# Two edits in a two-block transformer kernel: the order of ScalarE's copies in the within-chunk stage, and position scores of two heads on half the rows each

## The chip, the cores and the metric

The kernel runs on one core of a Trainium2 chip. The metric is the device time of one execution in microseconds (us), median of three runs. One further execution was profiled; all rows of the trace come from it.

## What is computed

The reference is a pair of transformer blocks on 256 tokens of width 2048, all in float32. The first block runs two layers of convolution and windowed attention. The second has a RWKV-7 mixer (16 heads of 64) beside a multi-head latent attention (8 heads), an output projection, and a gated feed-forward network. The two edited stages are the latent attention and a part of the RWKV mixer:

```python
# latent attention, 8 heads: 128 content dimensions and 64 position dimensions
sc = (einsum('bqhd,bkhd->bhqk', q_nope[:, q0:q1], k_nope[:, :q1])
      + einsum('bqhr,bkr->bhqk', q_pe[:, q0:q1], k_pe[:, :q1])) * scale
p = softmax(where(causal, sc, NEG_INF))
out = einsum('bhqk,bkhd->bqhd', p, v[:, :q1])
# RWKV-7: one step a token
sa = einsum('bhvk,bhk->bhv', state, a_t)
state = state * w_t + sa * b_t + v_t * k_t
out_t = einsum('bhvk,bhk->bhv', state, r_t)
```

The kernel computes the RWKV recurrence in chunks of 32 tokens: within a chunk the recurrence becomes a triangular system that is solved ahead, and a few small products; then a short chain over 8 chunks carries the state.

## The kernel before

The program is one long sequence of stages. Each stage gives every engine its own list of instructions, and an engine goes through its lists without stopping between stages; order across engines comes from semaphores alone, each counted upwards and written by hand (`wait_ge`, `then_inc`). Nothing plans the order but the code itself. Most stages stream weights in units of 128x2048 float32: SyncE loads a unit, ScalarE rounds it (line 229), VectorE or GpSimd forms the rest (lines 234, 241), and TensorE multiplies both parts.

**Latent attention** (`phase_mla`, lines 1722 to 1830). A head's scores lie in one PSUM bank, `1 + h % 3`, so three heads can be there at once: 128 columns for the first 128 queries, 256 for the second. TensorE's `scores(h)` (lines 1744 to 1752) makes for each query block one product of the content part (line 1750, 128 rows) and one of the position part (line 1751). The rotated position keys are 64 dimensions; the position queries of two heads share the 128 rows of one tile (`qT[:, 8 + h // 2]`), so the keys stand in `k_pad` twice, for even heads on rows 0 to 63 and for odd heads on rows 64 to 127, and the other half is zero. Then:

- VectorE, `biased(h)`: waits for head h's scores and for the transposes of head h-2 (its buffer `smm` is used by turns), scales and masks (line 1804), takes maxima (lines 1806, 1807) and negates them (line 1808);
- ScalarE: exponentials and their sums (lines 1783, 1784);
- VectorE, `finished(h)`: reciprocals and normalisation (lines 1813 to 1815);
- TensorE: three transposes (line 1765), which ScalarE copies (line 1793), and the output product (line 1775), which VectorE stores (line 1819).

TensorE's list is: scores of heads 0 and 1, and then for n from 0: scores of head n+2, transposes of head n, output of head n-1. VectorE's list is `biased(n + 1)`, `finished(n)`, `store(n - 2)`. `scores(h)` waits from head 3 on until `biased(h - 3)` has read the bank.

**Within-chunk stage** (`phase_within`, lines 1838 to 2001). There are 16 items: 8 pairs of heads by 2 halves of the sequence. For item n TensorE does, in this order: the products `G` (line 1915), the four transposes of the tokens of item n+1 into bank 2 (line 1860), the solved products `aq` (line 1923, into bank 5), the scores of item n+1 (line 1871: three products for each of two heads, on 64 rows each), the outputs that use `aq` (lines 1932, 1934, 1936), and the small products of the four chunks (lines 1945, 1947, 1949). ScalarE copies `G` (line 1974), moves `held` to `step_n` for item n-1 (`step_out`, line 1968, which waits for VectorE), copies the tokens of item n+1 out of bank 2 (`tokens_read`, lines 1961 to 1963), and copies `aq` (line 1980). VectorE masks the scores (line 1878), reads bank 5 (lines 1990, 1991), and reads the small products (lines 1997, 1999).

Of the kernel before, what the change touches and what calls it, by code (L numbers as in the profile page):

```python
# [10 lines left out]
ACT = mybir.ActivationFunctionType  # L11
AX = mybir.AxisListType

P = 128
# [14 lines left out]
MLA_H, NOPE, ROPE, VH = 8, 128, 64, 128  # L29
# [116 lines left out]
def program(nc, xT, pT, weights, params, sinks, rel_bias, lora, positions, consts, onehot, band_mask, masks, inv_freq, table, chunk_mats, out):  # L146
    ctx = ExitStack()
    with ctx:
# [1577 lines left out]
        def phase_mla(u_next, following):  # L1726
            scale = (NOPE + ROPE) ** -0.5
            stage = Stage()

            @stage.gpsimd  # L1730
            def _(pool):
                pool.wait_ge(mm_done.sem, u_next)
                pool.memset(lower[:, 16:32, :], 0.0).then_inc(mx["cleared"].sem, 1)

            @stage.sync
            def _(sp):
                sp.wait_ge(*mx["cleared"](1))
                for c in range(4):
                    sp.dma_start(lower[32 * c:32 * c + 32, :, 32 * c:32 * c + 32],
                                 chunk_mats[32 * c:32 * c + 32, :, :].rearrange("i s t -> s i t")).then_inc(mx["sol_in"].sem, 16)  # L1740

            @stage.tensor
            def _(pe):
                def scores(h):
                    if h >= 3:
                        pe.wait_ge(*ml["biased"](h - 2))
                    for qb in range(2):
                        n = P + P * qb
                        dst = ps[:, 1 + h % 3, P * qb:P * qb + n]
                        pe.matmul(dst, qT[:, h, P * qb:P * qb + P], kT[:, h, 0:n], start=True, stop=False)  # L1750
                        mm = pe.matmul(dst, qT[:, 8 + h // 2, P * qb:P * qb + P], k_pad[:, h % 2, 0:n], start=False, stop=True)
                    mm.then_inc(ml["scores"].sem, 1)

                pe.wait_ge(ev_done.sem, u_next + 2)
                scores(0)
                scores(1)
                for n in range(MLA_H + 1):
                    if n + 2 < MLA_H:
                        scores(n + 2)
                    if n < MLA_H:  # L1760
                        pe.wait_ge(*ml["normed"](n + 1))
                        if n >= 2:
                            pe.wait_ge(*ml["probsT_read"](n - 1))
                        for x in range(3):
                            mm = pe.transpose(ps[:, 4 + n % 2, x * P:x * P + P], smm[:, n % 2, x, :], ident[:, :])
                        mm.then_inc(ml["probsT"].sem, 1)
                    if n == MLA_H:
                        following.first_products(pe)
                    if n >= 1:
                        h = n - 1  # L1770
                        pe.wait_ge(*ml["probsT_read"](h + 1))
                        if h >= 2:
                            pe.wait_ge(*ml["stored"](h - 1))
                        for x, (q, k) in enumerate(((0, 0), (1, 0), (1, 1))):
                            mm = pe.matmul(ps[:, 6 + h % 2, q * P:q * P + P], vM[:, k, h * P:h * P + P], pTm[:, h % 2, x, :], start=k == 0, stop=k == q)
                        mm.then_inc(ml["outT"].sem, 1)

            @stage.scalar
            def _(act):
                def exps(h):  # L1780
                    s = st[:, h % 3, :]
                    act.wait_ge(*ml["biased"](h + 1))
                    act.activation(smm[:, h % 2, 0, :], smm[:, h % 2, 0, :], ACT.Exp, bias=s[:, 4:5], accum_out=s[:, 8:9])
                    act.activation(smm[:, h % 2, 1:3, :], smm[:, h % 2, 1:3, :], ACT.Exp, bias=s[:, 5:6], accum_out=s[:, 9:10]).then_inc(ml["exps"].sem, 1)

                exps(0)
                for h in range(MLA_H):
                    if h + 1 < MLA_H:
                        exps(h + 1)
                    act.wait_ge(*ml["probsT"](h + 1))  # L1790
                    if h >= 2:
                        act.wait_ge(*ml["outT"](h - 1))
                    act.activation(pTm[:, h % 2, :, :], ps[:, 4 + h % 2, 0:3 * P].rearrange("p (x k) -> p x k", x=3), ACT.Copy).then_inc(ml["probsT_read"].sem, 1)

            @stage.vector
            def _(v):
                link = dve_chain.start(v)

                def biased(h):
                    s = st[:, h % 3, :]  # L1800
                    v.wait_ge(*ml["scores"](h + 1))
                    if h >= 2:
                        v.wait_ge(*ml["probsT"](h - 1))
                    link(v.scalar_tensor_tensor(smm[:, h % 2, :, :], ps[:, 1 + h % 3, 0:3 * P].rearrange("p (x k) -> p x k", x=3), scale,
                                                causal[:, :, :], ALU.mult, ALU.add))
                    v.tensor_reduce(s[:, 0:1], smm[:, h % 2, 0, :], axis=AX.X, op=ALU.max)
                    link(v.tensor_reduce(s[:, 1:2], smm[:, h % 2, 1:3, :].rearrange("p x k -> p (x k)"), axis=AX.X, op=ALU.max))
                    v.tensor_scalar(s[:, 4:6], s[:, 0:2], -1.0, None, ALU.mult).then_inc(ml["biased"].sem, 1)

                def finished(h):  # L1810
                    s = st[:, h % 3, :]
                    v.wait_ge(*ml["exps"](h + 1))
                    link(v.reciprocal(s[:, 10:12], s[:, 8:10]))
                    v.tensor_scalar(smm[:, h % 2, 0, :], smm[:, h % 2, 0, :], s[:, 10:11], None, ALU.mult)
                    v.tensor_scalar(smm[:, h % 2, 1:3, :], smm[:, h % 2, 1:3, :], s[:, 11:12], None, ALU.mult).then_inc(ml["normed"].sem, 1)

                def store(h):
                    v.wait_ge(*ml["outT"](h + 1))
                    v.tensor_copy(y_mla[:, h, :], ps[:, 6 + h % 2, 0:T]).then_inc(ml["stored"].sem, 1)

                v.wait_ge(*mx["causal_in"](32))
                biased(0)
                for n in range(MLA_H + 2):
                    if n + 1 < MLA_H:
                        biased(n + 1)
                    if n < MLA_H:
                        finished(n)
                    if n == MLA_H:
                        following.first_mask(v)
                    if n >= 2:  # L1830
                        store(n - 2)
                link.end()
            return stage
# [8 lines left out]
        def phase_within(u_next):  # L1842
# [110 lines left out]
            @stage.scalar  # L1953
            def _(act):
                def tokens_read(n):
                    pair, sc = items[n]
                    y = n % 2
                    act.wait_ge(*wi["tok"](n + 1))
                    if n >= 2:
                        act.wait_ge(*wi["mn"](2 * (n - 1)))  # L1960
                    act.activation(tokA[:, y, :, 0:DH], ps[:, 2, 0:P].rearrange("p (h d) -> p h d", h=2), ACT.Copy)
                    act.activation(tokV[:, y, :], ps[:, 2, P:2 * P], ACT.Copy)
                    act.activation(chunk_ends[:, pair, sc, :, :], ps[:, 2, 2 * P:4 * P].rearrange("p (x d) -> p x d", x=2), ACT.Copy).then_inc(wi["tok_read"].sem, 1)

                def step_out(n):
                    pair, sc = items[n]
                    act.wait_ge(*wi["mn_read"](2 * n + 2))
                    act.activation(step_n[:, pair, sc, :, :], held[:, :, :], ACT.Copy).then_inc(wi["held"].sem, 1)

                tokens_read(0)  # L1970
                for n, (pair, sc) in enumerate(items):
                    y = n % 2
                    act.wait_ge(*wi["G"](n + 1))
                    act.activation(tokA[:, y, :, DH:P], ps[:, 5, 0:P].rearrange("p (h d) -> p h d", h=2), ACT.Copy).then_inc(wi["G_read"].sem, 1)
                    if n:
                        step_out(n - 1)
                    if n + 1 < len(items):
                        tokens_read(n + 1)
                    act.wait_ge(*wi["aq"](n + 1))
                    act.activation(aq[:, y, :, :], ps[:, 5, P:3 * P].rearrange("p (h d) -> p h d", h=2), ACT.Copy).then_inc(wi["aq_read"].sem, 1)  # L1980
                step_out(len(items) - 1)

            @stage.vector
# [487 lines left out]
```

## Time and profile before

| what | value |
|---|---|
| median of three runs | 2248.16 us (2246.68 to 2249.49) |
| the profiled execution | 2245.08 us, of which 2243.3 us are the span of the profile |
| TensorE products, busy | 2197.8 us (98%), 14609 instructions |
| TensorE weight loads, busy | 1930.5 us (86%) |
| VectorE, busy | 1698.2 us (76%) |
| ScalarE, busy | 1068.6 us (48%) |
| GpSimd, busy | 550.0 us (25%) |
| latent attention | from 1260 to 1288 us of the span |
| within-chunk stage | from 1288 to 1357 us |

Two thirds of the span are the large products of the two blocks; the chain that ended last runs through TensorE for 86% of it. The two edited stages are 4% of the span. In rows of the timeline the first number is the start in us from the span's start, the second the duration in us; PE is TensorE's products, PEld its weight loads, DVE is VectorE, ACT is ScalarE. A float32 product appears as two records. A bracket gives the idle time of that engine just ahead and what ended it.

### The profile page before, as it was taken

Reading aid. Unit: us, or ns where it says so; the run is one execution under the profiler, and the core shown is the slowest. Engines: PE = TensorE matmul, PEld = TensorE weight load, DVE = VectorE, ACT = ScalarE, POOL = GpSimd, SP = SyncE. Lnnn points to the kernel's source line nnn. Section 1 sums busy time; section 2 is a strip of 40 time slices with the busy share of each in tenths; the row PEclk is TensorE's granted clock in tenths of the full one; section 3 lists DMA queues with packets and bytes.
Section 4 is the critical chain, followed back from the end, with each engine's and each line's share of the span. In section 5 each row is a group of like instructions: output and inputs, shape, how many; then the busy total and the mean of one; then the engine's idle time right before and its main releaser. Section 6 shows DMA issues by size and latency. Waiting matters only on the chain.

```text
span 2243.3 us, 38851 instructions
## 1 busy us (share of the span) xinstructions
PE 2197.8 (98%) x14609; PEld 1930.5 (86%) x14609; DVE 1698.2 (76%) x2879; ACT 1068.6 (48%) x1427; POOL 550.0 (25%) x226
## 2 busy tenths in 40 slices
PE   7999999999999999999999899999999999999997
PEld 6888888888888888899999887888888888888886
DVE  7688678885888588788878766788888885447886
ACT  5444464444545564556644633444444443334444
POOL 4676631018676530210001322100000000000011
PEclk9999999999999999999999999999999999999998
DMA  7445445555545355554445300555555555555554
GB/s 253 172 175 176 146 170 188 188 187 189 183 165 173 142 186 182 187 193 170 159 150 186 113 3 21 188 185 187 186 188 187 187 186 189 188 186 189 187 207 167
DMA packets 69032, 384.89 MB, mean 172 GB/s; under 512 B 15088, under 2 KB 22768, under 8 KB 23984
## 3 DMA queue, kind: packets, MB, share of 16 engines
q1 hardware_dynamic: 68912, 383.22, 48.3%
q8 instruction: 84, 1.38, 0.2%
q14 instruction: 36, 0.29, 0.0%
HBM read 380.02 MB, written 3.18 MB: 171 GB/s over the span
## 4 chain that ended last, share of the span: by engine, by line
PE 86%; DVE 5%; issue 3%; ACT 2%; POOL 1%; DMA 1%; SPq 0%; DVEq 0%; POOLq 0%; ACTq 0%
PE ps L259 44%; PE ps L260 24%; PE ps L262 3%; PE ps L247 3%; PE ps L248 2%; PE ps L249 2%; PE ps L878 1%; DVE low L234 1%; PE ps L859 1%; POOL ssq L1139 1%; DMA raw<-weights_dram 1%; PE ps L867 1%; DVE step_m L1997 1%; ACT whi L229 0%; PE ps L913 0%
## 5 line engine op out<-in xcount | busy, mean ns | idle before, releaser
L259 PE MATMUL ps<-opA,whi 128*128 128x512 f32 x2460 | 871.9, 395 | 0.3 <-DVE low L234 0.3
L260 PE MATMUL ps<-opA,low 128*128 128x256 f32 x2624 | 706.7, 279 | 0.2 <-DVE opA L996 0.2
L229 ACT ACTIVATE whi<-raw 128x2048 fp32r<-128x2048 f32 x346 | 660.2, 1909 | 76.3 <-DMA raw<-weights_dram 74.7
L234 DVE TENSOR_TENSOR low<-raw,whi 128x2048 fp32r<-128x2048 f32 x252 | 577.1, 2291 | 66.7 <-ACT whi L229 50.6
L259 PEld LDWEIGHTS ps<-opA,whi 128*128 128x128 f32 x2460 | 461.0, 187 | 106.2 <-issue 2.8
L241 POOL TENSOR_TENSOR low<-raw,whi 128x2048 fp32r<-128x2048 f32 x95 | 436.7, 4606 | 440.5 <-ACT whi L229 414.1
L259 PE MATMUL ps<-opB,whi 128*128 128x512 f32 x1380 | 497.1, 400 | 16.2 <-DVE opB L408 11.7
L260 PEld LDWEIGHTS ps<-opA,low 128*128 128x128 f32 x2624 | 492.0, 188 | 14.3 <-DVE opA L996 0.5
L260 PE MATMUL ps<-opB,low 128*128 128x256 f32 x1472 | 398.5, 281 | 0.0
L259 PEld LDWEIGHTS ps<-opB,whi 128*128 128x128 f32 x1380 | 260.9, 189 | 80.5 <-DVE low L402 10.4
L268 ACT ACTIVATE crossed<-ps 128x256 f32<-128x256 f32 x168 | 64.6, 384 | 513.7 <-PE ps L262 513.5
L260 PEld LDWEIGHTS ps<-opB,low 128*128 128x128 f32 x1472 | 278.7, 189 | 7.3
L717 DVE SCALAR_TENSOR_TENSOR ps<-a_in,par,ps 128x256 f32<-128x256 f32 x464 | 226.8, 489 | 14.6
L259 PE MATMUL ps<-act_hl,whi 128*128 128x512 f32 x672 | 236.5, 393 | 0.0
L1135 POOL MEMSET ssq<- 128x256 f32 (+1 forms) x4 | 1.5, 366 | 807.2 <-DVE t L988 677.1
L260 PE MATMUL ps<-act_hl,low 128*128 128x256 f32 x704 | 191.4, 279 | 0.0
L247 PE MATMUL ps<-opB,whi 128*128 128x256 f32 x560 | 161.8, 289 | 0.2 <-DVE ps L1442 0.2
L249 PE MATMUL ps<-opB,low 128*128 128x256 f32 x560 | 158.8, 284 | 0.0
L248 PE MATMUL ps<-opB,whi 128*128 128x256 f32 x560 | 158.5, 283 | 0.0
L259 PEld LDWEIGHTS ps<-act_hl,whi 128*128 128x128 f32 x672 | 125.9, 187 | 28.6
L260 PEld LDWEIGHTS ps<-act_hl,low 128*128 128x128 f32 x704 | 131.9, 187 | 2.9
L1139 POOL TENSOR_TENSOR ssq<-ssq,sq 128x256 f32<-128x256 f32 (+1 forms) x64 | 65.4, 1021 | 247.5 <-ACT sq L1052 182.6
(390 smaller groups left out, 2661.8 us busy)
## 6 DMA issues: line engine op xcount, KB each, us to landing
raw<-weights_dram SPq DMA_DIRECT2D x350, 1024.0 KB, 4.8
bias_t<-table_dram SPq DMA_DIRECT2D x16, 384.0 KB, 5.8
hT<-xT_dram SPq DMA_DIRECT2D x4, 512.0 KB, 9.0
out_dram<-hT SPq DMA_DIRECT2D x4, 512.0 KB, 2.9
lora_g<-lora_dram SPq DMA_DIRECT2D x1, 1024.0 KB, 4.9
p_in<-pT_dram SPq DMA_DIRECT2D x2, 256.0 KB, 5.1
lora_wa<-lora_dram SPq DMA_DIRECT2D x1, 512.0 KB, 5.6
chunk_mats_dram<-compact SPq DMA_DIRECT2D x4, 128.0 KB, 3.1
```

Source lines behind the costliest of these rows:

```text
L229: act.activation(whi[:, v % RING, :], raw[:, v % RING, :], ACT.Copy).then_inc(hi_done.sem, 1)
L234: v_.tensor_tensor(wlo(v % RING, 0, width), raw[:, v % RING, 0:width], whi[:, v % RING, 0:width].bitcast(F32), ALU.subtract).then_inc(lo_d ...
L241: pool.tensor_tensor(wlo(v % RING), raw[:, v % RING, :], whi[:, v % RING, :].bitcast(F32), ALU.subtract).then_inc(lo_done.sem, 1)
L247: pe.matmul(dst, whi[:, s, w0:w0 + P], op[:, k, 0:T], start=start, stop=False)
L248: pe.matmul(dst, whi[:, s, w0:w0 + P], op[:, k, T:2 * T], start=False, stop=False)
L249: return pe.matmul(dst, wlo(s, w0, w0 + P), op[:, k, 0:T], start=False, stop=stop)
L259: pe.matmul(*cross, start=start, stop=False)
L260: mm = pe.matmul(ps[:, b, 0:T], wlo(s, w0, w0 + P), op[:, k, 0:T], start=False, stop=False)
L262: mm = pe.matmul(*cross, start=False, stop=True)
L268: act.activation(crossed[:, b, :], ps[:, b if bank is None else bank, T:2 * T], ACT.Copy).then_inc(read.sem, 1)
L717: link(v.scalar_tensor_tensor(y, taps, w, y, ALU.mult, ALU.add))
L1139: pool.tensor_tensor(total, total, part, ALU.add).then_inc(summed.sem, 1)
```

## The change

In latent attention TensorE's `scores` now makes two heads in one piece: the content products of both, then the position products of both, each of these on the 64 rows that hold the head's queries and keys, and one signal for the pair. A pair is issued at even steps only. VectorE's wait counts pairs. In the within-chunk stage ScalarE's copy of `aq` stands ahead of the token copies of the next item.

```diff
             def _(pe):
-                def scores(h):
-                    if h >= 3:
-                        pe.wait_ge(*ml["biased"](h - 2))
+                def scores(pair):
+                    for h in (2 * pair, 2 * pair + 1):
+                        if h >= 3:
+                            pe.wait_ge(*ml["biased"](h - 2))
                     for qb in range(2):
                         n = P + P * qb
-                        dst = ps[:, 1 + h % 3, P * qb:P * qb + n]
-                        pe.matmul(dst, qT[:, h, P * qb:P * qb + P], kT[:, h, 0:n], start=True, stop=False)
-                        mm = pe.matmul(dst, qT[:, 8 + h // 2, P * qb:P * qb + P], k_pad[:, h % 2, 0:n], start=False, stop=True)
+                        dst = [ps[:, 1 + (2 * pair + x) % 3, P * qb:P * qb + n] for x in range(2)]
+                        for x in range(2):
+                            pe.matmul(dst[x], qT[:, 2 * pair + x, P * qb:P * qb + P], kT[:, 2 * pair + x, 0:n], start=True, stop=False)
+                        for x in range(2):
+                            r = slice(64 * x, 64 * x + 64)
+                            mm = pe.matmul(dst[x], qT[r, 8 + pair, P * qb:P * qb + P], k_pad[r, x, 0:n], start=False, stop=True)
                     mm.then_inc(ml["scores"].sem, 1)
 
                 pe.wait_ge(ev_done.sem, u_next + 2)
                 scores(0)
-                scores(1)
                 for n in range(MLA_H + 1):
-                    if n + 2 < MLA_H:
-                        scores(n + 2)
+                    if n % 2 == 0 and n + 2 < MLA_H:
+                        scores(n // 2 + 1)
...
                 def biased(h):
                     s = st[:, h % 3, :]
-                    v.wait_ge(*ml["scores"](h + 1))
+                    v.wait_ge(*ml["scores"](h // 2 + 1))
...
                     if n:
                         step_out(n - 1)
+                    act.wait_ge(*wi["aq"](n + 1))
+                    act.activation(aq[:, y, :, :], ps[:, 5, P:3 * P].rearrange("p (h d) -> p h d", h=2), ACT.Copy).then_inc(wi["aq_read"].sem, 1)
                     if n + 1 < len(items):
                         tokens_read(n + 1)
-                    act.wait_ge(*wi["aq"](n + 1))
-                    act.activation(aq[:, y, :, :], ps[:, 5, P:3 * P].rearrange("p (h d) -> p h d", h=2), ACT.Copy).then_inc(wi["aq_read"].sem, 1)
                 step_out(len(items) - 1)
```

## Rows read from the trace of the kernel before

**Rows 1.** Waits, both stages: engine and line, releaser: us in total, times, longest

```profile
PEld ps L1932 <- ACT aq L1980: 4.6, 15, 0.4
```

**Rows 2.** Timeline of a steady item of the within-chunk stage

```profile
1320.32 0.96 DVE L1878 TENSOR_TENSOR scm<-ps,msk 128x768 f32<-128x768 f32 x1 [1.32 <-PE ps L1871]
1320.38 0.20 PEld L1932 LDWEIGHTS ps<-scm,aq 128*64 128x64 f32 x4 [0.30 <-ACT aq L1980]
...
1321.51 0.28 DVE L1991 COPY kk<-ps 128x128 f32<-128x128 f32 x1
...
1321.95 0.52 PEld L1915 LDWEIGHTS ps<-tokV,scm 128*128 128x128 f32 x4
...
1322.97 0.71 PE L1923 MATMUL ps<-tokA,lower 128*128 128x128 f32 x4
...
1323.32 0.42 ACT L1968 ACTIVATE step_n<-held 128x256 f32<-128x256 f32 x1 [0.40 <-DVE held L1999]
1323.61 0.30 PEld L1871 LDWEIGHTS ps<-uS,a_gate 64*128 64x128 f32 x4
...
1324.16 0.39 PE L1871 MATMUL ps<-uS 64*128 64x128 f32 x4
1324.22 0.40 ACT L1980 ACTIVATE aq<-ps 128x256 f32<-128x256 f32 x1
...
1324.66 0.20 PEld L1932 LDWEIGHTS ps<-scm,aq 128*64 128x64 f32 x4 [0.30 <-ACT aq L1980]
```

**Rows 3.** Timeline of the first item and the start of the second

```profile
1288.97 0.71 PE L1923 MATMUL ps<-tokA,lower 128*128 128x128 f32 x4
...
1290.16 0.39 PE L1871 MATMUL ps<-uS 64*128 64x128 f32 x4
1290.48 0.20 PEld L1932 LDWEIGHTS ps<-scm,aq 128*64 128x64 f32 x4
...
1291.67 0.28 DVE L1991 COPY kk<-ps 128x128 f32<-128x128 f32 x1
...
1292.06 0.52 PEld L1915 LDWEIGHTS ps<-tokV,scm 128*128 128x128 f32 x4
...
1293.09 0.71 PE L1923 MATMUL ps<-tokA,lower 128*128 128x128 f32 x4
```

**Rows 4.** Timeline of the start of latent attention, heads 0 and 1

```profile
1260.35 0.49 PE L1750 MATMUL ps<-kT,qT 128*128 128x128 f32 x2 [0.65 <-DVE small L1619]
...
1260.67 0.39 PE L1751 MATMUL ps<-k_pad,qT 128*128 128x128 f32 x2
...
1260.89 0.60 PE L1750 MATMUL ps<-kT,qT 128*128 128x256 f32 x2
...
1261.33 0.59 PE L1751 MATMUL ps<-k_pad,qT 128*128 128x256 f32 x2
...
1262.04 0.56 DVE L1804 SCALAR_TENSOR_TENSOR smm<-ps,causal 128x384 f32<-128x384 f32 x1 [1.75 <-PE ps L1751]
...
1263.28 0.17 DVE L1808 TENSOR_SCALAR st<-st 128x2 f32<-128x2 f32 x1
...
1265.46 0.31 PEld L1765 LDWEIGHTS ps<-ident,smm 128*128 128x128 f32 x3 [1.32 <-DVE smm L1815]
```

**Rows 5.** Timeline of two later heads

```profile
1268.23 0.31 PEld L1765 LDWEIGHTS ps<-ident,smm 128*128 128x128 f32 x3 [1.31 <-DVE smm L1815]
...
1269.29 0.39 PE L1750 MATMUL ps<-kT,qT 128*128 128x128 f32 x2
...
1271.00 0.31 PEld L1765 LDWEIGHTS ps<-ident,smm 128*128 128x128 f32 x3 [0.64 <-DVE smm L1815]
```

**Rows 6.** Busy by stretch: PE, PEld, DVE, ACT, POOL busy (instructions), PEclk granted clock, DMA share, GB/s

```profile
1401.00:1405.00 4.00, 1.79 (x10) 1.09 (x8) 3.93 (x8) 1.87 (x3) 0.00 (x0) 0.97 0.02 4
1405.00:1411.00 6.00, 5.70 (x17) 4.53 (x18) 3.18 (x7) 1.04 (x3) 0.00 (x0) 0.50 0.00 0
1278.00:1282.00 4.00, 2.28 (x15) 1.63 (x14) 3.45 (x13) 1.63 (x6) 1.02 (x2) 1.00 0.00 0
```

## The prediction

> **What bounds the kernel now.** I began with the page: TensorE is busy nearly everywhere, so outside the two edited stages the change can only move things in time. The stages are short: latent attention runs from about 1260 to 1288 us of the span, the within-chunk stage from there to 1357. I then asked who waits for whom in them, and read the timeline of one steady item, of the first item, and of the first heads.
>
> The waits name the target of the first edit: TensorE's weight loads of line 1932 wait for ScalarE's copy of `aq` 15 times, 4.6 us in all [rows 1]. The steady item shows why. The item repeats every 4.28 us (line 1932 at 1320.38 and at 1324.66). The solved products of line 1923 end at 1322.97 + 0.71 = 1323.68, but their copy (line 1980) starts only at 1324.22, because ScalarE first does `step_out` (line 1968, from 1323.32, held back by VectorE's `held`) and then three token copies. TensorE has meanwhile finished the next scores (1324.16 + 0.39 = 1324.55) and stands until 1324.66 [rows 2].
>
> In latent attention the chain is another one. One head follows another every 2.77 us (line 1765 at 1268.23 and 1271.00), and each time the transposes wait for VectorE's normalised probabilities; the bracket of the second row still has 0.64 us of idle load time [rows 5]. VectorE's next head waits for the transposes in turn, so VectorE, ScalarE's exponentials and three transposes make the cycle and the score products hide inside it. At the very start they don't: VectorE's line 1804 begins at 1262.04, when the scores of head 0, begun at 1260.35, are done [rows 4].
>
> **Edit 1, the order of ScalarE's copies.** Nothing is added or removed; three token copies move behind the `aq` copy. In the new order the `aq` copy can start once `step_out` is over (1323.32 + 0.42 = 1323.74) and the products have ended (1323.68), so it ends near 1324.13, 0.4 us before the scores do. ScalarE's wait for `aq` now stands ahead of the token copies. Who needs those: line 1915 of the next item, 1.57 us after line 1932 (1320.38, 1321.95) [rows 2]. The three copies take at most 0.9 us (1323.32 to 1324.22 holds them and line 1968), so they end by 1325.0; line 1915 then comes at 1324.48 + 1.57 = 1326.05, a microsecond later. Nothing new stalls there.
>
> What TensorE gets is not the whole idle time. After the last score product (64 rows of the array) comes line 1932 (128 rows, 64 columns), and the first item shows this step without a wait, since there `step_out` does not exist yet: last score group at 1290.16, line 1932 at 1290.48, 0.32 apart; in the steady item 1324.16 and 1324.66, 0.50 apart [rows 2, 3]. So 0.18 us an item is to be had and the rest belongs to the switch. The first item's own period agrees: line 1923 at 1288.97 and 1293.09, 4.12 against 4.28 [rows 2, 3].
>
> Would VectorE then take over? Line 1915 waits for its line 1991, which in the steady item ends at 1321.79, 1.47 after the mask of line 1878 began at 1320.32; line 1915 follows at 1321.95 [rows 2]. If that stayed, only 0.10 of the 0.18 would come. But in the first item, with line 1932 early, line 1991 runs from 1291.67 to 1291.95 and line 1915 starts at 1292.06, 1.58 after line 1932 as in the steady item (1.57), so VectorE isn't in the way [rows 3]. I take 0.18. It counts for items 2 to 14; item 1 has about half (its old period was shorter), item 0 had no wait, item 15 has no next tokens and no change. 13 x 0.18 + 0.09 = **2.4 us gained**. Bounds: 0 if something else takes the place, 4.6 if the whole wait goes.
>
> **Edit 2, scores two heads at a time.** Counts first. The 32 products stay 32; 16 of them (the position part) now use 64 rows each, two side by side. A 128-column product takes 0.22 us of the array (1260.67 to 1260.89), a 256-column one 0.44 (1260.89 to 1261.33) [rows 4]. A pair of heads is now 2 x 2 x (0.22 + 0.44) = 2.64 us. In the within-chunk scores, the same form (two heads on 64 rows each, two banks), a pair of 128-column products fits in one slot: three pairs start at 1323.61 and the last group starts at 1324.16, 0.11 + 2 x 0.22 later [rows 2]. So the new pair needs 1.32 for the 128-row products and 0.66 for the position products: 1.98.
>
> Against that stand changes of the array's form: 128 to 64 rows and back, twice a pair. Their price is in the steady item: line 1923's last product ends at 1323.68, lasting 0.28, so it began at 1323.40 and the next could have begun at 1323.51; line 1871's load begins at 1323.61 and is not hidden, which costs another 0.11 [rows 2]. That is 0.21, I take 0.20; four of them are 0.80. The pair costs **2.78 us against 2.64**: the side by side gains nothing on TensorE. The Trainium skill (TensorEngine Tiling, Theoretical Speedup) gives up to 2x for dimensions of at most 64, by which the pair would be 1.98 us; the same page says under Key Properties that a change of tiling mode drains the array. The rows above decide for the drain here.
>
> The larger cost is one of order: a pair's scores are signalled together, and TensorE does a pair in one piece at even steps.
> - Start: head 0's scores are ready after the whole pair. 0.11 for the first load, 1.98, three inner switches and the last record's tail: about 2.85 after 1260.35, at 1263.20 in place of 1261.92. Line 1804 moves from 1262.04 to 1263.32: **+1.28**.
> - Pair 1 must wait until head 0's biased scores have been read out of its bank (line 1808, 1263.28 + 0.17 + 1.28 = 1264.73) and then stands ahead of the first transposes. It starts at 1264.79 and lets the transposes go at 1264.79 + 2.78 = 1267.57. Before, they went at 1265.46 [rows 4]: 2.11 late, **0.83** beyond the start's share. What is queued behind TensorE's wait is just this: head 0's transposes, for which VectorE waits.
> - Pairs 2 and 3: the score products start 1.06 after a head's transposes (1268.23, 1269.29) [rows 5]. With 2.67 behind them (2.78 less the hidden first load) the next transposes go at 3.73 in place of 2.77: **0.96 each, 1.92**. At odd steps nothing is inserted and the 2.77 holds; that time doesn't give it back, as the chain runs through the transposes.
>
> Sum: 1.28 + 0.83 + 1.92 = **4.0 us lost**. Bounds: were the switches free, the start would cost 0.66, pair 1 another 0.14 and pairs 2 and 3 0.16 each, 1.1 together; were the 64-row pairs not side by side, each of the four pairs adds 0.66, 6.7 together. One signal a pair instead of two is nothing beside that. The zeroed half of `k_pad` is still written; its fill is unchanged. No queue but TensorE's and VectorE's waits is touched by this edit, and no DMA is moved.
>
> **Sum against the profile.** +4.0 - 2.4 = +1.6 us. The profiled execution took 2245.08 us (span 2243.3), 3.1 under the median of 2248.16; it would become 2246.7, and the median **2249.8**. A measurement of this kernel can tell about 0.2%, 4.5 us, from no change.
>
> **Rivals.**
> - *The clock falls* (chance 0.20). Between head 0's transposes and head 1's TensorE will now stand idle for about 2.2 us (2.77 less 0.55 of work), soon after 1.6 us of idling for pair 1. Of 4 us with 1.79 busy at 1401 the trace shows the end at a granted clock falling to 0.50, 1.2 GHz, and six busy microseconds stay there; 4 us with 2.28 busy at 1278 kept 1.00 [rows 6]. The new stretch from 1267 to 1271 has some 1.8 busy. At half clock, the transposes, the output products and pair 2 (0.33 + 0.66 + 1.98) take 3.0 longer on the path: +4.6, **2252.8**, slower than before. It decides only if the fall comes before pair 2. The Trainium skill (TensorE: Matmul & The Clock Gate, Part 1) has it that idling throttles and activity releases; that agrees with these rows.
> - *The 64-row pairs do not overlap* (0.08): +6.7 - 2.4 = +4.3, **2252.5**. Against: the score groups of line 1871.
> - *Edit 1 gives nothing* (0.10), VectorE's reads or the later token copies setting the same 4.28: +4.0, **2252.2**. Against: the first item.
> - *Switches cheap* (0.12): 1.1 - 2.4 = -1.3, **2246.9**. For it: a load of another row group might start early; against: the load of line 1871 begins only 0.07 before the recorded end of line 1923 [rows 2].
> - The case of the sum keeps 0.50.
>
> A gain over 0.2% would need 4.5 us, practically all of the wait and no loss in attention: 0.03. A loss over 0.2% is the clock case's upper part and pieces of the two before it: 0.17. The range takes in the rivals' times and the spread of the median: 2245.5 to 2254.0.
>
> **What would show it.** Right: in attention line 1804 first starts 1.2 to 1.4 us after its old place, and head-to-head distances alternate between about 2.8 and 3.7; line 1751 appears as 64-row groups; attention ends some 4 us later. In the within-chunk stage line 1932's wait for `aq` is gone but for item 15, the period is 4.10, and 16 items end 2.4 us nearer to their start. Wrong: a new wait before line 1915 or 1974, a period still at 4.28, distances in attention of 2.77 throughout, or a granted clock under 1.00 between 1260 and 1360.

## The result, and the profile after

The kernel after takes 2251.46 us, median of 20 runs (2248.67 to 2254.66). In the same series of runs the kernel before took 2246.49 us. The ratio is 1.0021, with a 95% interval of 1.0015 to 1.0028: 4.7 us slower, just over what the prediction called tellable. The profiled execution took 2250.74 us, its span 2248.9 us. The prediction started from 2248.16 us for the kernel before, the median of three runs; the 2246.49 is that of 20.

The page shows the same busy time on every engine as before within 4 us, so the loss is time in which TensorE waits or runs slowly:

```profile
span 2248.9 us, 38853 instructions
...
PE 2198.7 (98%) x14609; PEld 1930.6 (86%) x14609; DVE 1698.0 (76%) x2879; ACT 1072.2 (48%) x1427; POOL 548.5 (24%) x226
```

The waits of both stages (line numbers are three higher in the kernel after: 1926 was 1923, 1935 was 1932, 1768 was 1765). The first row is of the kernel before, the others are of the kernel after:

```profile
DVE smm L1804 <- PE ps L1765: 2.9, 6, 0.7
DVE smm L1807 <- PE ps L1768: 8.8, 6, 3.1
...
PEld ps L1752 <- DVE st L1811: 2.0, 1, 2.0
PEld ps L1755 <- issue: 1.9, 5, 0.7
...
PEld ps L1935 <- ACT aq L1981: 0.4, 1, 0.4
```

The last row answers to [rows 1]: 4.6 us in 15 waits became 0.4 in one, that of the last item. The others are new or larger: VectorE waits 8.8 us for transposes where it waited 2.9, and TensorE's loads wait once 2 us for bank 1. Ahead of five position products the loads stand idle for a time that the profile puts down to nothing; there the array changes its form, from products on 128 rows to products on 64.

A steady item of the within-chunk stage, to be held against [rows 2]:

```profile
1322.09 0.52 PEld L1918 LDWEIGHTS ps<-tokV,scm 128*128 128x128 f32 x4
...
1323.12 0.71 PE L1926 MATMUL ps<-tokA,lower 128*128 128x128 f32 x4
1323.44 0.42 ACT L1971 ACTIVATE step_n<-held 128x256 f32<-128x256 f32 x1 [0.38 <-DVE held L2002]
...
1323.87 0.39 ACT L1981 ACTIVATE aq<-ps 128x256 f32<-128x256 f32 x1
...
1324.31 0.39 PE L1874 MATMUL ps<-uS 64*128 64x128 f32 x4
...
1324.62 0.20 PEld L1935 LDWEIGHTS ps<-scm,aq 128*64 128x64 f32 x4
...
1325.82 0.28 DVE L1994 COPY kk<-ps 128x128 f32<-128x128 f32 x1
1326.21 0.52 PEld L1918 LDWEIGHTS ps<-tokV,scm 128*128 128x128 f32 x4
```

ScalarE's copy of the solved products ends at 1324.26, and line 1935 follows the scores by 0.31 us (1324.31, 1324.62) instead of 0.50. The item repeats after 4.12 us (1322.09, 1326.21). VectorE's line 1994 ends at 1326.10, 0.11 us ahead of the next line 1918, and no wait for it is on the list.

Latent attention's start and first transposes, to be held against [rows 4]:

```profile
1261.24 0.71 PE L1752 MATMUL ps<-kT,qT 128*128 128x128 f32 x4 [0.67 <-DVE small L1619]
1261.88 0.30 PEld L1755 LDWEIGHTS ps<-k_pad,qT 64*128 64x128 f32 x4
...
1262.30 1.13 PE L1752 MATMUL ps<-kT,qT 128*128 128x256 f32 x4
...
1263.36 0.30 PEld L1755 LDWEIGHTS ps<-k_pad,qT 64*128 64x128 f32 x4 [0.33 <-issue]
...
1264.19 0.56 DVE L1807 SCALAR_TENSOR_TENSOR smm<-ps,causal 128x384 f32<-128x384 f32 x1 [3.01 <-PE ps L1755]
...
1265.65 0.52 PEld L1752 LDWEIGHTS ps<-kT,qT 128*128 128x128 f32 x4 [1.99 <-DVE st L1811]
...
1266.88 2.07 PE L1752 MATMUL ps<-kT,qT 128*128 128x256 f32 x4
...
1268.89 1.18 PE L1755 MATMUL ps<-k_pad,qT 64*128 64x256 f32 x4
...
1270.00 0.31 PEld L1768 LDWEIGHTS ps<-ident,smm 128*128 128x128 f32 x3 [0.61 <-issue]
...
1272.77 0.31 PEld L1768 LDWEIGHTS ps<-ident,smm 128*128 128x128 f32 x3 [2.46 <-DVE smm L1818]
```

The first mask now comes 2.95 us after the first score (before: 1.69). Pair 0 takes what was reckoned, but pair 1 does not: its 256-column content products last 2.07 us where pair 0's lasted 1.13, and its position products 1.18. The busy time by stretch says why. Its columns are those of [rows 6]; the granted clock is the number ahead of the last two:

```profile
1261.00:1265.00 4.00, 2.83 (x16) 1.80 (x16) 0.84 (x5) 1.18 (x1) 1.44 (x1) 1.00 0.78 268
1265.00:1270.00 5.00, 4.34 (x16) 2.56 (x17) 2.42 (x10) 1.98 (x8) 0.00 (x0) 0.66 1.00 104
1270.00:1273.00 3.00, 0.78 (x7) 0.54 (x6) 1.95 (x7) 1.39 (x5) 0.00 (x0) 1.00 0.00 0
1273.00:1277.00 4.00, 4.00 (x20) 3.44 (x19) 2.28 (x8) 1.57 (x6) 0.00 (x0) 0.57 0.01 2
...
1290.00:1294.00 4.00, 3.50 (x17) 3.50 (x18) 1.92 (x7) 1.81 (x6) 0.00 (x0) 0.57 0.02 4
```

TensorE fell to half its clock, 1.2 GHz, three times between 1266 and 1294 us: in pair 1, in pair 2, and in the last output products. In the execution profiled before, the whole of both stages ran at 1.00:

```profile
1260.00:1360.00 100.00, 93.23 (x1561) 77.17 (x1561) 65.34 (x245) 41.12 (x139) 21.24 (x20) 1.00 0.11 29
```

### The profile page after: what moved, and what is told of

Same layout as the page of the kernel before. It is cut to its first block, busy times and chain, and to the rows that moved or that the text cites. A ratio compares the mean times of both kernels' runs of the same rounds, so it can differ in the third digit from the quotient of the medians.

```text
span 2248.9 us, 38853 instructions
## 1 busy us (share of the span) xinstructions
PE 2198.7 (98%) x14609; PEld 1930.6 (86%) x14609; DVE 1698.0 (76%) x2879; ACT 1072.2 (48%) x1427; POOL 548.5 (24%) x226
## 4 chain that ended last, share of the span: by engine, by line
PE 88%; DVE 4%; issue 3%; ACT 2%; POOL 1%; DMA 1%; SPq 0%; POOLq 0%; DVEq 0%; ACTq 0%
PE ps L259 44%; PE ps L260 24%; PE ps L262 3%; PE ps L247 3%; PE ps L248 2%; PE ps L249 2%; PE ps L878 1%; DVE low L234 1%; PE ps L859 1%; POOL ssq L1139 1%; DMA raw<-weights_dram 1%; PE ps L867 1%; PE ps L1874 1%; PE ps L1926 0%; PE ps L1918 0%
```

## Where the time went, by milestones

Each row is read from the timeline of one profiled execution; times are in us from the first score of attention. "Distances" are those of the loads of the transposes, head 0 to head 7. "Attention" is the time to item 0's solved products (line 1923 before), and "items" the time from there to the last `step_out`. "Kept busy" means that TensorE is given products that nobody needs in its idle stretches of attention (see e4).

| kernel | first mask | head 0's transposes | distances | attention | items |
|---|---|---|---|---|---|
| before | 1.69 | 5.11 | 2.77 2.77 2.76 2.77 3.22 2.77 1.15 | 28.62 | 68.09 |
| after | 2.95 | 8.76 | 2.77 5.27 2.77 3.71 3.21 2.77 1.77 | 37.13 | 66.00 |
| e1, copy order alone | 1.69 | 5.11 | 2.77 2.77 2.77 2.76 3.23 2.76 1.77 | 29.99 | 65.97 |
| e2, pairs alone | 2.95 | 7.17 | 2.76 5.29 2.77 3.71 3.22 3.12 1.76 | 36.02 | 68.19 |
| e3, pairs, full rows | 3.00 | 6.98 | 2.92 3.46 2.93 3.46 3.37 2.77 1.77 | 35.03 | 65.99 |
| e4, pairs, kept busy | 2.95 | 7.17 | 2.77 3.71 2.76 3.71 3.22 2.77 1.16 | 32.57 | 65.99 |
| e5, copy order, kept busy | 1.69 | 5.12 | 2.77 2.76 2.77 2.77 3.22 2.78 1.15 | 28.65 | 65.98 |
| e6, first heads single, kept busy | 1.69 | 5.91 | 2.77 3.71 2.76 3.71 3.22 2.77 1.16 | 31.31 | 65.96 |
| e7, 64 rows, one head | 2.28 | 6.40 | 2.76 3.04 3.04 3.04 3.22 2.77 1.15 | 30.72 | 65.97 |
| e8, full rows, kept busy | 3.00 | 6.97 | 2.93 3.46 2.92 3.47 3.38 2.77 1.16 | 32.36 | 65.97 |
| e9, as e5 in these stages | 1.69 | 5.11 | 2.77 2.77 2.77 2.77 3.22 2.77 1.16 | 28.63 | 65.97 |
| e10, e1 again | 1.69 | 5.11 | 2.76 2.77 2.76 2.77 3.22 2.77 1.15 | 28.63 | 65.97 |
| e11, pairs, busy at the start only | 2.95 | 7.17 | 2.76 3.71 2.76 3.71 3.22 2.77 1.77 | 33.89 | 65.97 |

So attention lost 8.5 us in the profiled execution (37.13 against 28.62), and the items gave 2.1 back (68.09, 66.00). That is 6.4 us more, while the two spans differ by 5.6 (2248.9 and 2243.3). The normalisation stage behind them gave about 1.2 back, since the clock fell there in the execution before ([rows 6]) and not in the one after; the account of e9 has the numbers. The experiments had to tell how the 8.5 divides into the order in pairs, the array's changes of form, and the clock.

Each ratio below is to runs of the kernel before in the same series, whose medians were 2246.49 us for the kernel after, 2246.75 for e1 to e4, 2247.28 for e5 to e8 and 2247.23 for e9 to e11. Ratios of different series can be compared, the medians only roughly. Most experiments have 10 or 11 runs, e2 has 5.

| kernel | ratio to before, 95% interval | median us |
|---|---|---|
| after | 1.0021 (1.0015 to 1.0028) | 2251.46 |
| e1, copy order alone | 0.9994 (0.9985 to 1.0003) | 2245.35 |
| e10, the same again | 0.9996 (0.9986 to 1.0005) | 2245.09 |
| e2, pairs alone | 1.0038 (1.0024 to 1.0051) | 2254.05 |
| e3, pairs, full rows | 1.0022 (1.0012 to 1.0031) | 2251.05 |
| e4, pairs, kept busy | 1.0008 (0.9999 to 1.0017) | 2248.56 |
| e11, pairs, busy at the start only | 1.0018 (1.0009 to 1.0027) | 2250.99 |
| e6, first heads single, kept busy | 0.9998 (0.9989 to 1.0007) | 2246.71 |
| e8, full rows, kept busy | 1.0008 (0.9999 to 1.0017) | 2248.89 |
| e7, 64 rows, one head at a time | 0.9999 (0.9990 to 1.0008) | 2246.53 |
| e5, copy order, kept busy | 0.9988 (0.9978 to 0.9997) | 2243.89 |
| e9, e5 and the norm stage kept busy | 0.9984 (0.9975 to 0.9993) | 2242.99 |

## The experiments

### e1 and e10: the copy order alone

The kernel before with only this edit:

```diff
+                    act.wait_ge(*wi["aq"](n + 1))
+                    act.activation(aq[:, y, :, :], ...)
                     if n + 1 < len(items):
                         tokens_read(n + 1)
-                    act.wait_ge(*wi["aq"](n + 1))
-                    act.activation(aq[:, y, :, :], ...)
```

> Edit 1 alone (ScalarE copies the solved products ahead of the next tokens; attention as before). Theory: the within-chunk items go from 4.28 to 4.12 us apart as in the kernel after, the stage is 2.1 us shorter and the whole kernel 2 us faster than before (ratio 0.9991). Rival: the shorter items only came with what the attention edit shifted, and the items stay at 4.28: no change. In attention the distance of the transposes stays 2.77 us and the granted clock 1.00.

> Edit 1 alone once more, for its interval beside e5 and e9 on the same chip. Theory: 2.1 us from the within-chunk stage, ratio 0.9991; the granted clock may fall at the end of attention, as it did in e1's trace. If e5 is really faster than this, the unneeded products in attention are worth about 1 us in the median.

The items are 4.12 us apart in both traces and the items' time is 65.97 us, 2.1 less than before. The rival, that the edit needs what attention shifted, is out. The ratios of 0.9994 and 0.9996 have the forecast 0.9991 in their intervals, and 1.0 too: the whole kernel's time alone would not have settled this; the items do. In e1's execution the clock fell at the end of attention, in the old order of heads:

```profile
1263.00:1285.00 22.00, 17.39 (x112) 14.28 (x112) 16.41 (x58) 11.29 (x36) 2.73 (x3) 1.00 0.30 73
1285.00:1289.00 4.00, 3.50 (x18) 3.50 (x19) 1.92 (x7) 1.80 (x6) 0.00 (x0) 0.57 0.02 4
```

It cost 1.4 us of attention (29.99 against 28.62). The same kernel as e10 had no fall there, nor had the execution of before:

```profile
1258.00:1300.00 42.00, 36.69 (x421) 30.80 (x421) 28.41 (x100) 19.09 (x64) 16.91 (x19) 1.00 0.18 39
```

The fall is a matter of the execution, not only of the kernel.

### e2: the pairs alone

The kernel after with ScalarE's two lines back in the old order.

> Edit 2 alone (pairs of heads, position products on 64 rows; ScalarE's order as before). If the two edits simply add: before plus 5.0 plus 2.1, so about 7 us slower (ratio 1.0031), with the first output products of the within-chunk stage 8 to 9 us later after the first score than before. Rival, the edits interact (edit 1 gave more because of what edit 2 left late): the loss is only about 5 us.

The ratio is 1.0038, the loss 8.5 us; 7 lies in the interval, 5 (ratio 1.0022) does not. So the edits add, as far as five runs can tell. The wait of edit 1 is back at its old size, and attention was hit by the clock twice:

```profile
PEld ps L1935 <- ACT aq L1983: 4.7, 15, 0.4
```

```profile
1271.00:1274.40 3.40, 3.40 (x13) 2.17 (x11) 1.74 (x8) 0.99 (x4) 0.00 (x0) 0.50 0.01 2
...
1284.60:1291.40 6.80, 5.68 (x26) 5.39 (x27) 3.88 (x14) 2.95 (x10) 0.00 (x0) 0.50 0.01 2
```

The first low stretch lies in pair 2 and makes the distance from head 1's to head 2's transposes 5.29; the same distance from head 3 to head 4, with pair 3 at full clock, is 3.71.

### e4: the pairs, with TensorE kept busy

```diff
                 scores(0)
+                pe.wait_ge(hi_done.sem, u_next + 1)
+                gaps = (0, 8, 0, 6, 0, 6, 6, 0)
+                following.keep_running(pe, 6, 0)
...
                     if n < MLA_H:
+                        following.keep_running(pe, gaps[n], 0)
                         pe.wait_ge(*ml["normed"](n + 1))
```

`keep_running` is the kernel's own: it multiplies weights that are there into a bank that nobody reads.

> The kernel after, with TensorE fed unneeded 512-column products (0.22 us each, into a free bank) in its idle stretches of attention: 6 after the first pair, 8 ahead of head 1's transposes, 6 ahead of those of heads 3, 5 and 6. Theory (half of attention's 8.5 us is the clock at 1.2 GHz): the granted clock stays at 1.00 from 1260 to 1300 us, the transposes go 2.8, 3.7, 2.8, 3.7 apart, attention loses 4.0 to 4.5 us against before, and the whole kernel ends about 2 us slower than before (ratio 1.0009), 3 faster than the kernel after. Rival (the order alone makes the loss): the time stays 5 us over before.

This run separates the clock from the rest. The loads of the transposes, and the stretch of both stages' border:

```profile
1267.85 0.31 PEld L1772 LDWEIGHTS ps<-ident,smm 128*128 128x128 f32 x3 [0.33 <-issue]
1270.62 0.31 PEld L1772 LDWEIGHTS ps<-ident,smm 128*128 128x128 f32 x3 [0.80 <-DVE smm L1822]
...
1274.33 0.31 PEld L1772 LDWEIGHTS ps<-ident,smm 128*128 128x128 f32 x3 [0.33 <-issue]
1277.09 0.31 PEld L1772 LDWEIGHTS ps<-ident,smm 128*128 128x128 f32 x3 [0.60 <-DVE smm L1822]
```

```profile
1260.00:1300.00 40.00, 38.02 (x336) 29.21 (x342) 24.10 (x80) 17.12 (x56) 10.88 (x17) 1.00 0.17 41
```

At a clock of 1.00 throughout, attention takes 32.57 us, 3.95 more than before; the sum had 4.03. The unneeded products cost nothing: the distances are 2.77 and 3.71 as in the undisturbed heads of the kernel after. The rest of the 8.5 us in the kernel after, 4.56, is the clock, in that execution. It divides into the three falls: 1.59 in pair 1 (head 0's transposes at 8.76 against 7.17), 1.56 in pair 2 (the distance of 5.27 against 3.71), and 1.40 behind head 6's transposes. By the ratios (1.0021 and 1.0008) it is 2.9 us. Their intervals just overlap, but e3 and e8 repeat the step (1.0022 and 1.0008), and the mean granted clock over all runs goes with it: 0.9930 for the kernel after and 0.9944 for e4, 0.9929 for e3 and 0.9941 for e8.

### e3 and e8: the pairs on full rows

```diff
-                            r = slice(64 * x, 64 * x + 64)
-                            mm = pe.matmul(dst[x], qT[r, 8 + pair, ...], k_pad[r, x, 0:n], ...)
+                            mm = pe.matmul(dst[x], qT[:, 8 + pair, ...], k_pad[:, x, 0:n], ...)
```

> The kernel after, but the position products use all 128 rows again, with the zero half of the keys; the order in pairs stays. Theory (the order is what costs, the 64 rows hardly matter): the first mask starts 2.9 us after the first score, the distance from head 1's to head 2's transposes is 3.6 us at full clock, and the kernel is within 1 us of the kernel after, about 4 us slower than before. Rival (the changes of the array's form are the loss): the distances fall to about 2.8 to 3.0 and the kernel comes within 1 us of before or beats it.

> The pairs on full rows (as e3), kept busy as e4. Theory: the order in pairs alone costs 3.5 us of attention (distances 2.8 and 3.6, clock 1.00), the 64 rows another 0.4; the kernel is 1.4 us slower than before and within 0.6 us of e4. Rival (the 64 rows are the loss): attention is within 1 us of before.

The 64 rows are nearly nothing either way. Kept busy, attention takes 32.36 us on full rows and 32.57 on half, and both kernels are at 1.0008. e3 and the kernel after are at 1.0022 and 1.0021. What costs is the order in pairs: 3.74 us without a single change of form, where I had expected 3.5. The distances come out less even than forecast, 2.93 and 3.46 for 2.8 and 3.6; on full rows the transposes' loads can start ahead of the last score product, so their records stand some 0.15 us earlier behind a pair (head 0's load at 1269.73 in e8, its product at 1269.95; in e4 both at 1267.85). In e3 the clock fell once, after the last pair, and for longer:

```profile
1259.00:1284.00 25.00, 17.00 (x112) 14.88 (x112) 15.75 (x55) 11.19 (x36) 2.81 (x3) 1.00 0.34 64
1284.00:1291.00 7.00, 5.68 (x28) 5.36 (x30) 2.66 (x11) 2.66 (x9) 0.00 (x0) 0.54 0.01 2
```

### e7: 64 rows without the pairs

```diff
-                        mm = pe.matmul(dst, qT[:, 8 + h // 2, ...], k_pad[:, h % 2, 0:n], ...)
+                        r = slice(64 * (h % 2), 64 * (h % 2) + 64)
+                        mm = pe.matmul(dst, qT[r, 8 + h // 2, ...], k_pad[r, h % 2, 0:n], ...)
```

This stands in the order of before, with edit 1 in place.

> Edit 1, and attention in the order of before (one head at a time), but with the position product on the 64 rows of its head: the changes of the array's form without the pairing. By 0.2 us a change, a head's scores take 2.1 us instead of 1.3. The first mask comes 2.3 us after the first score, the transposes are about 3.2 us apart while scores are made (2.77 at the end), attention is about 3 us longer than before, and the kernel 1 us slower than before. If a change costs nothing the distances are 2.77 and it equals edit 1 alone.

It measures a change of form by itself. The loads of one head, content and position in turn:

```profile
1266.99 0.30 PEld L1750 LDWEIGHTS ps<-kT,qT 128*128 128x128 f32 x2
1267.42 0.29 PEld L1752 LDWEIGHTS ps<-k_pad,qT 64*128 64x128 f32 x2
1267.83 0.30 PEld L1750 LDWEIGHTS ps<-kT,qT 128*128 128x128 f32 x2
1268.46 0.29 PEld L1752 LDWEIGHTS ps<-k_pad,qT 64*128 64x128 f32 x2 [0.33 <-issue]
```

The steps are 0.43, 0.41 and 0.63 us, where 128 columns cost 0.22 and 256 cost 0.44 without a change: 0.19 to 0.21 for each. The Trainium skill (TensorEngine Tiling, Key Properties) says that a change of tiling mode drains TensorE; these rows agree and give the price. The first mask at 2.28 is as forecast. The distances are 3.04 and not 3.2: I had added 1.06 and 2.1 and forgotten that the transposes' first load is hidden, which the sum of the prediction has. So attention is 2.1 us longer and not 3, edit 1 gives 2.1, and the ratio is 0.9999 where I expected 1 us more than before.

### e6: the first two heads single

The kernel e4 with `scores(0)` replaced by the two single heads of before, each with its own signal.

> The kernel after, kept busy as in e4, but heads 0 and 1 are made singly as before and only heads 2 to 7 in pairs. Theory (the start's share is 1.28 us): the first mask starts 1.69 us after the first score, the first transposes at 5.9 instead of 7.2, later distances 2.8 and 3.7 as in e4; attention 2.7 us longer than before, the kernel 1.3 us faster than e4, about 0.5 us slower than before. Rival: the wait for bank 1 swallows the gain and the first transposes stay near 7.

First mask 1.69, first transposes 5.91, attention 31.31, 2.69 more than before: each as forecast. The kernel's ratio of 0.9998 has the 0.5 us that I expected over before in its interval. The start's share of the pairs' loss is 32.57 - 31.31 = 1.26 us, and 1.9 of what is left are the two distances of 3.71.

### e11: kept busy at the start only

The kernel e4 with `gaps = (0, 8, 0, 0, 0, 0, 0, 0)`.

> The kernel after, kept busy only in the two long idle stretches at its start: 6 unneeded products after the first pair, 8 ahead of head 1's transposes; not ahead of those of heads 3, 5 and 6. Theory as predicted (the idle time around the first transposes is what drops the clock): most of e4's 3 us comes back, 2 to 3 us slower than before, heads 1 to 4 at the distances 3.7 and 2.8, with at most a fall after head 5. Rival (the later gaps, 1.5 to 1.7 us each, do as much): falls appear between heads 3 and 6 or at the stage's end and the time stays 4 us or more over before.

In the profiled execution the theory held: distances 2.76, 3.71, 2.77, 3.71, and one fall, as head 6's transposes are due (1286.32):

```profile
1260.00:1286.00 26.00, 20.63 (x126) 14.97 (x126) 16.47 (x58) 11.36 (x37) 2.62 (x3) 1.00 0.27 61
1286.00:1289.50 3.50, 3.17 (x15) 3.17 (x16) 1.75 (x7) 1.44 (x6) 0.00 (x0) 0.51 0.02 5
```

But that execution took 2246.9 us, 4 less than the median of its runs. The median of 2250.99 is nearer to the kernel after (2251.46) than to e4 (2248.56), while the interval of 1.0018 overlaps both. So the time is the rival's. The mean granted clock was 0.996 in the profiled execution and 0.993 or 0.994 in the ten others, so those ran some 10 us longer at half clock (an estimate: 0.002 to 0.003 of the span, twice over). Where they did is not known, as no trace of such a run was taken. The later gaps are one candidate; in the profiled execution they were 1.55, 2.00 and 1.55 us long ahead of heads 3, 5 and 6, not 1.5 to 1.7. The normalisation stage is the other: it had no fall in e11's profiled execution, and had one or two in those of most other kernels (table under e9).

### e5 and e9: a version that beats both

e5 is e1 with `gaps = (2, 4, 1, 1, 1, 1, 6, 0)` in the old order of heads. e9 also keeps TensorE busy in the normalisation stage:

```diff
                     early_products(pe, u_next, n, range(8, 16), op)
+                pe.wait_ge(*no["var"](2))
+                following.keep_running(pe, 5, 2)
```

and three more such products ahead of the third block of the output projection's first unit.

> Edit 1 alone, attention in the order of before, with TensorE fed unneeded products in the idle stretches that this order has (2 ahead of head 0's transposes, 4 of head 1's, one each of heads 2 to 5, 6 of head 6). Theory: the distances stay 2.77 us, no clock falls between 1260 and 1300 us, and where the run before loses the clock at the end of attention this one does not: 2 to 3.5 us faster than before, a little faster than edit 1 alone. Rival: the extra products get in the way of the transposes and it is slower than edit 1 alone.

> The kernel of e5, with TensorE also kept busy in the normalisation stage's two longest waits near 1402 and 1403 us (5 unneeded products ahead of the output projection's first product, 3 ahead of its third block), where the traces of before, e5 and others show the granted clock at 0.50 for 6.8 us. Theory (that fall costs half of its stretch, up to 3.4 us): no fall between 1380 and 1430 us, 2 to 3.4 us faster than e5 (ratio about 0.9975 against before). Rival: the products there are hidden or the fall only moves: no change from e5.

e5 is 2.7 us faster than before (0.9988, interval 0.9978 to 0.9997), with attention at 28.65 and no fall; so it beats both kernels. The difference from e1 and e10 (0.9994, 0.9996) is of the expected size and not told apart by the intervals. In e9 the fall near 1403, which e5 still has, is gone (a short one at 1383 stands in both):

```profile
1403.00:1410.00 7.00, 5.98 (x17) 4.80 (x18) 4.14 (x10) 1.64 (x3) 0.00 (x0) 0.54 0.06 9
```

```profile
1395.00:1420.00 25.00, 22.16 (x119) 18.06 (x118) 19.35 (x32) 14.56 (x18) 4.19 (x4) 1.00 0.43 165
```

The first row is e5, the second e9. The time follows by less than I expected: 0.9984 against 0.9988, 0.9 us that the intervals don't tell apart, and not 2 to 3.4 us. The traces have the 0.9 us too, and where the rest goes. At full clock TensorE meets VectorE's low halves of the operand sooner and waits for them:

```profile
1403.92 0.49 PE L259 MATMUL ps<-opB,whi 128*128 128x512 f32 x1 [0.21 <-DVE opB L2188]
...
1405.85 0.50 PE L259 MATMUL ps<-opB,whi 128*128 128x512 f32 x1 [0.96 <-DVE opB L2188]
```

Even so e9 is 1.9 us ahead of e5 by VectorE's line 1101 (1410.87 in e9, 1412.74 in e5). It gives 1.0 back at the next wait for the low half of a weight unit; the first row is e5, the second e9:

```profile
1418.43 0.19 PEld L259 LDWEIGHTS ps<-opB,whi 128*128 128x128 f32 x1 [0.85 <-DVE low L234]
1417.53 0.19 PEld L259 LDWEIGHTS ps<-opB,whi 128*128 128x128 f32 x1 [1.82 <-DVE low L234]
```

All profiled executions together give the price of the falls in this stage. The time is that from VectorE's last copy of `held` in the within-chunk stage (1356.82 us in the kernel before) to the same instruction of its line 1101 in the output projection (1471.03 there):

| falls in between, us after the start | executions | time, us |
|---|---|---|
| none | after, e1, e11 | 112.95 to 113.09 |
| at 48 to 49, for 6.8 | before, e7 | 114.21, 114.26 |
| at 29, for 3.4 | e9 | 114.61 |
| both of these | e2, e3, e4, e5, e6, e10 | 115.54 to 115.97 |
| at 29, for 6.8 | e8 | 116.13 |

The later fall costs 1.2 us, the earlier one 1.5. This is also why e4's execution, 4.56 us ahead of the kernel after's in attention, ends only 2.1 ahead of it by the spans (2246.8 and 2248.9): e4 had both falls here, worth 2.7, and the kernel after none.

## Why the prediction was right or wrong

The range held the time and the case with the largest chance did not come. The forecast had +1.6 us and 2249.8; measured were +4.7 by the ratio, which by the bound of 0.2% counts as slower, a case given 0.17. That the range held says little, as it reached from faster than before to above every rival. And the time of 2249.8 is nearer to the 2251.46 than the difference is, because it was added to a median of three runs that lay 1.7 us high.

**Edit 1.** Right in mechanism and size. 4.12 us an item where the sum had 4.10 at full effect, 2.1 us in place of 2.4. The step from the scores to line 1935 became 0.19 shorter, and the other steps of the item 0.03 longer in all. The first item of the trace of before had shown both the price of the switch ahead of line 1932 (0.32 there, 0.31 now) and the free VectorE. The rival "edit 1 gives nothing" is out by e1, e10 and the items of every other run that has the edit; e2, without it, kept 4.7 us of waits.

**Edit 2, the sum.** Right, term by term, once the clock is held (e4). Start: 1.28 reckoned, 1.26 measured. First transposes: 2.11 late reckoned, 2.06 measured (7.17 against 5.11). Pairs 2 and 3: distances of 3.73 reckoned, 3.71 measured. Sum 4.03 reckoned, 3.95 measured. The split into order and form was right in the main: e8 has 3.74 of the 3.95 without any change of form. The 64 rows are left with 0.21, where the sum had 0.14 for each of four pairs. And e7 gives 0.19 to 0.21 for a change where the sum took 0.20. The rivals "no overlap" and "switches cheap" are out by the same numbers.

**The clock.** Here the step failed that weighed the rivals: a chance of 0.20 for the clock, and the sentence that it decides only if the fall comes before pair 2. The mechanism was the right one, and e4 shows it. But I looked at one gap, between head 0's and head 1's transposes, and gave that one a single fall. The profiled execution had three: in pair 1 after the wait for bank 1, which I had named only in passing, in pair 2, and in the last output products, where the pairs add nothing and where even the old order fell in e1. The rows for it stood in [rows 6]: the clock at 1405 fell behind two short waits, none of them as long as the one for bank 1 or those ahead of the transposes of heads 1, 3, 5 and 6 in the new order. A rival whose condition is met several times in a stage should have had about the chance of the main case. By the rows now known I would put the forecast at the sum of the two, 1.6 and about 3: +4.6. The price failed too. It put 3.0 us on one fall, as if transposes, output products and pair 2 all ran at half clock; the three falls of the trace cost 1.59, 1.56 and 1.40 us. That 3.0 is close to what keeping busy gave back by the ratios (2.9) is luck: it is the size of two such falls, and the profiled execution lost 4.6 to three. The Trainium skill (TensorE: Matmul & The Clock Gate, Part 1) says that activity releases the throttle; e4 agrees, as products that nobody needs keep the clock at 1.00.

**Left open.** How often each gap drops the clock was not measured; that needs many profiled executions of one kernel. Every stage time here is from one execution of its kernel. How much of the medians' distance between e4 and the kernel after lies at which gap is open for the same reason. The overlap of two 64-row products was not undone by itself.

## What to carry to other kernels

Putting two pieces of work together on the engine that is not the bound saves nothing there and makes the bounding chain wait for the second piece; ask of each batch who needs its first half. A product on half the rows has to pay for its change of form, 0.2 us each way here, while two 128-column products side by side save 0.22. By these prices several such products must follow each other, as in this kernel's within-chunk scores; that is an estimate, no run varied their number. When an edit lengthens the idle stretches of TensorE in a latency-bound stage, reckon with the clock, and try filling the gaps with products that nobody reads: in attention they left the distances as they were, and in the kernels with pairs they gave back about 3 us. In the order of before no gain from them is told apart (e5 against e1 and e10).

## What the runs showed of the hardware

- Two executions of one and the same program differ in where TensorE's clock falls: e1 had a granted clock of 0.57 from 1285 to 1289, e10, the same kernel, 1.00 from 1258 to 1300. A single profile tells what one execution met; the runs of one kernel spread over 3 to 10 us here, and falls like these, at 1.2 to 1.6 us each, can be a part of that.
- A fall does not need a long idle stretch. The first one of the kernel after came behind a gap in the products from 1264.07 to 1265.65, 1.6 us, and the one at 1405 in the kernel before behind gaps of 1.33 and 0.90 us.
- A fall costs less than half of its stretch where TensorE also waits for others: in the normalisation stage one of 6.8 us cost 1.2 us (114.2 against 113.0), while in attention one of 3.4 us cost 1.4 to 1.6.
- After 256-column products a change to 64 rows leaves the load of weights idle for 0.33 us, yet the step is 0.63 us in e7, only 0.19 more than the 0.44 without a change. Idle time of the loads is no measure of what a change costs.
